# Gate and up products of a feed-forward layer: nine of eleven steps by seven block products in place of eight

## The reference, cut to what matters

```python
D_FF = 2816
h2 = rms_norm_2(x, g_ffn[layer])                              # 512 x 1024
x = x + (jax.nn.silu(h2 @ w_ffn_gate[layer])                  # 1024 x 2816
         * (h2 @ w_ffn_up[layer])) @ w_ffn_down[layer]
return rms_norm_2(x, g_final)
```

## Time and profile before

| | |
|---|---|
| median of 3 runs | 1060.87 us (1060.67 to 1061.41) |
| the profiled execution | 1061.1 us |
| its span, from first to last instruction | 1059.3 us |
| PE busy in the span | 1049.7 us |
| DVE, ACT, POOL busy | 509.0, 448.8, 400.2 us |
| mean granted TensorE clock | 0.999 of full speed |

### The profile page before, as it was taken

The page is one execution under the profiler, slowest core; times in us unless marked ns, Lnnn a source line. Parts: engine busy times, 40 slices in busy tenths (PEclk is TensorE's granted clock), DMA queues, the critical chain, the costliest instruction groups (busy, mean ns, idle before and its releaser), DMA issues.

```text
span 1059.3 us, 14455 instructions
## 1 busy us (share of the span) xinstructions
PE 1049.7 (99%) x5545; PEld 844.1 (80%) x5545; DVE 509.0 (48%) x1061; ACT 448.8 (42%) x788; POOL 400.2 (38%) x300
## 2 busy tenths in 40 slices
PE   9999999999999999999999999999999999999997
PEld 8877897767678876888777888888888888888886
DVE  6766788875752316998587344230000000032444
ACT  6444457676653425233465414342221221233533
POOL 3455520001025333446000255434435354465772
PEclk9999999999999999999999999999999999999999
DMA  9541141201032331332221232223232323323221
GB/s 298 184 120 51 34 119 41 75 17 44 28 120 80 72 117 43 101 99 80 80 80 41 80 104 95 91 77 110 80 118 79 114 84 104 114 80 100 82 97 80
DMA packets 84724, 95.72 MB, mean 90 GB/s; under 512 B 8121, under 2 KB 70930, under 8 KB 84666
## 3 DMA queue, kind: packets, MB, share of 16 engines
q1 hardware_dynamic: 83706, 92.46, 28.0%
q0 software_dynamic: 560, 2.12, 0.6%
q10 hardware_dynamic: 400, 0.35, 0.1%
HBM read 92.80 MB, written 2.12 MB: 90 GB/s over the span
## 4 chain that ended last, share of the span: by engine, by line
PE 94%; DVE 4%; ACT 1%; issue 1%; POOL 0%; DVEq 0%; ACTq 0%; POOLq 0%
PE bank L1882 56%; PE bank L2194 23%; PE bank L1940 4%; PE bank L1971 3%; PE bank L2012 3%; PE bank L1988 1%; DVE L L1478 1%; PE bank L2169 1%; PE bank L1833 1%; PE bank L2098 1%; PE bank L2045 1%; DVE L L1524 1%; DVE pool L1483 0%; PE bank L2001 0%; PE bank L1964 0%
## 5 line engine op out<-in xcount | busy, mean ns | idle before, releaser
L1042 POOL TENSOR_TENSOR w_lo<-raw,w_hi 128x512 fp32r<-128x512 f32 (+1 forms) x190 | 267.2, 1436 | 415.7 <-ACT w_hi L1104 403.0
L1882 PE MATMUL bank<-h_hi,w_hi 128*128 128x512 f32 (+1 forms) x560 | 224.0, 400 | 0.3 <-ACT h_hi L1315 0.2
L1882 PE MATMUL bank<-h_hi,w_lo 128*128 128x512 f32 (+1 forms) x560 | 218.6, 390 | 0.0
L1882 PE MATMUL bank<-h_lo,w_hi 128*128 128x512 f32 (+1 forms) x560 | 217.8, 390 | 0.0
L1082 POOL TENSOR_TENSOR w_lo<-raw,w_hi 128x512 fp32r<-128x512 f32 x88 | 110.7, 1290 | 133.5 <-ACT w_hi L1353 67.1
L1104 ACT ACTIVATE w_hi<-raw 128x512 fp32r<-128x512 f32 (+3 forms) x94 | 111.2, 1213 | 116.1 <-PE bank L1882 113.8
L1882 PE MATMUL bank<-w_hi,h_hi 128*128 128x512 f32 (+2 forms) x397 | 145.3, 366 | 0.0
L1882 PE MATMUL bank<-w_lo,h_hi 128*128 128x512 f32 (+2 forms) x397 | 144.5, 364 | 0.0
L1882 PE MATMUL bank<-w_hi,h_lo 128*128 128x512 f32 (+2 forms) x397 | 144.5, 364 | 0.0
L2194 PE MATMUL bank<-h_hi,w_hi 128*128 128x512 f32 x352 | 137.1, 389 | 0.0
L2194 PE MATMUL bank<-h_hi,w_lo 128*128 128x512 f32 x352 | 137.0, 389 | 0.0
(11 more groups left out here) (213 smaller groups left out, 1260.3 us busy)
## 6 DMA issues: line engine op xcount, KB each, us to landing
raw<-in_w_in SPq DMA_DIRECT2D x29, 1024.0 KB, 5.3
raw<-in_w_ffn_gate SPq DMA_DIRECT2D x11, 1024.0 KB, 5.4
raw<-in_w_ffn_up SPq DMA_DIRECT2D x11, 1024.0 KB, 5.4
raw<-in_w_out SPq DMA_DIRECT2D x8, 1024.0 KB, 5.0
raw<-in_w_ffn_down SPq DMA_DIRECT2D x8, 1024.0 KB, 5.1
raw<-in_w_in SPq DMA_DIRECT2D x8, 512.0 KB, 4.6
pool<-in_cmp_w SPq DMA_DIRECT2D x4, 1024.0 KB, 9.1
raw<-in_w_ffn_down SPq DMA_DIRECT2D x4, 768.0 KB, 4.3
```

The costliest lines, as they stand in the source:

```text
L1042: nc.gpsimd.tensor_tensor(w_lo[:, u.n % 2, cols], raw[:, u.n % 2, cols], w_hi[:, u.n % 2, cols].bitcast(F32), ALU.subtract).then_inc(lo_do ...
L1882: ins = mm(bank[t.bank][0:t.m, 0:u.width if u.token else T], stationary, moving, start=first and n == 0, stop=last and n == len(products) ...
```

## The change

Two of the eleven steps stay as they are ("plain", the first and the last). The nine between are made by Strassen's scheme in Winograd's form, seven block products in place of eight. For one step and one of the two matrices, the 1024 features are cut in halves, the 256 columns in two blocks of 128 and the 512 tokens in two halves of 256: a 2 x 2 product of blocks, eight products of (512 features x 128 columns) by (512 features x 256 tokens). The scheme forms four sums of weight blocks and four sums of token blocks, makes seven products and adds these up differently. Gate and up give 14 products a step, each 4 blocks of features x 3 = 12 matmuls with 256 moving columns. In detail:
- **Token sums**, once: DVE adds `h_hi` and `h_lo` to one array, forms four sums of blocks, ACT makes their high parts and DVE their low parts (`token_sums_of_h`, `token_low`).
- **Weight sums**, in each fast step: POOL makes eight sums of 512 columns (`weight_sums`), six of them in place in `raw`, two into `PT`.
- **High and low parts**: ACT makes 14 high parts of 512 columns a step (`high`), DVE all 14 low parts (`split_fast`); both go into rings of seven pieces in `w_hi` and `w_lo`, so they run up to seven products ahead of PE. POOL makes low parts in the plain steps only.
- **Loads**: weights lie in memory in blocks as the stage needs them (the host array is reordered); SP loads eight blocks of 256 KB a fast step, each as soon as the low part that was the last to read its place in `raw` is done.
- **Merging**: the products go to banks 0 to 7; ACT moves four of them to SBUF, DVE makes eight sums and three multiplications a step (`merge`), ACT three SiLUs.

The diff, cut to its core. The steps and the table of a fast step's products (matrix, weight block or `None` for the sum in `PT`, number of the product), and how many weight sums each needs:

```diff
+    PLAIN_STEPS = 2
+    FAST_STEPS = FFN_STEPS - PLAIN_STEPS
...
+        A11, A12, A21, A22 = range(4)
+        GATE, UP = range(2)
+        fast = [(GATE, A12, 2), (UP, A12, 2), (GATE, A11, 1), (UP, A11, 1), (GATE, A21, 5), (UP, A21, 5), (GATE, A11, 6), (UP, A11, 6),
+                (GATE, A12, 3), (GATE, None, 7), (UP, None, 7), (UP, A12, 3), (GATE, A22, 4), (UP, A22, 4)]
+        FAST, RING, MERGES, WEIGHT_SUMS = len(fast), 7, 11, 8
+        def sums_before(i):
+            return {4: 2, 5: 4, 6: 5, 7: 6, 8: 7, 9: 1, 10: 3, 11: 8}.get(i, 0)
```

SP's loads:

```diff
+            plain_load(0, 0)
+            for j in range(2):
+                sp.wait_ge(lo_done, order[n0 + j].lo_end)
+                for b in (A12, A11, A21, A22):
+                    load_block(0, j, b)
+            with sp.Fori(0, FAST_STEPS - 1) as f:
+                for i in (6, 7, 8, 11, 12, 13):
+                    j = fast[i][0]
+                    sp.wait_ge(*lo_at(f, i))
+                    for b in {6: (A21,), 7: (A21,), 8: (A12, A11), 11: (A12, A11), 12: (A22,), 13: (A22,)}[i]:
+                        load_block(f + 1, j, b)
```

POOL's sums:

```diff
+                        if i in (4, 5):
+                            for b in (A11, A21, A22):
+                                pool_e.wait_ge(block_in[j][b], f * 16 + 16)
...
+                            nc.gpsimd.tensor_tensor(PT[:, j, :], w11, w21, ALU.subtract).then_inc(weight_sum, 1)
+                            pool_e.wait_ge(weight_sum, n + (2 * j + 1))
+                            nc.gpsimd.tensor_tensor(w21, w21, w22, ALU.add).then_inc(weight_sum, 1)
+                        if i in (6, 7):
+                            pool_e.wait_ge(weight_sum, n + (2 * j + 2))
+                            pool_e.wait_ge(*lo_at(f, 2 + j))
+                            nc.gpsimd.tensor_tensor(w11, w21, w11, ALU.subtract).then_inc(weight_sum, 1)
+                        if i in (8, 11):
+                            pool_e.wait_ge(weight_sum, n + (5 + j))
+                            pool_e.wait_ge(*lo_at(f, j))
+                            nc.gpsimd.tensor_tensor(w12, w12, w11, ALU.subtract).then_inc(weight_sum, 1)
```

ACT's order in a fast step:

```diff
+                    def fast_step(f, last=False):
+                        for p in range(FAST):
+                            if p in (0, 1, 4, 5):
+                                sc.wait_ge(product_done, f * FAST + (p + 1))
...
+                            if p == 13:
+                                sc.wait_ge(product_done, f * FAST + 13)
+                                act_fn(L[:, 4, 0:256], bank[4][:, 0:256], ACT.Silu).then_inc(fast_silu, 1)
+                            if p + RING < FAST:
+                                high(f, p + RING)
+                            elif not last:
+                                high(f + 1, p + RING - FAST)
```

DVE's low parts, and their order among the merges:

```diff
+                    def split_fast(f, i):
+                        j, b, _ = fast[i]
+                        ve.wait_ge(fast_hi, f * FAST + (i + 1))
+                        v.tensor_tensor(ring(w_lo, i), weight_block(j, b), ring(w_hi, i).bitcast(F32), ALU.subtract)\
+                            .then_inc(fast_lo, 1)
...
+                        for p in range(FAST):
+                            merge(f, p)
+                            if p + RING < FAST:
+                                split_fast(f, p + RING)
+                            elif not last:
+                                split_fast(f + 1, p + RING - FAST)
```

PE's products:

```diff
+                    def fast_step(f):
+                        for i, (j, _, m) in enumerate(fast):
+                            pe.wait_ge(*lo_at(f, i))
+                            if i == 2:
+                                pe.wait_ge(fast_silu, f * 3 + 1)
+                            if i == 3:
+                                pe.wait_ge(merged_done, f * MERGES + 1)
...
+                            for k in range(4):
+                                for w, x in ((w_hi, x_hi), (w_hi, x_lo), (w_lo, x_hi)):
+                                    ins = mm(dst[:, 0:256], ring(w, i)[:, P * k:P * k + P], x[:, k, :],
+                                             start=n == 0 and m in (1, 2, 3, 5), stop=n == 11, skip_group_check=True)
```

More of the change, by code:

```diff
@@ new lines, in _ @@
+                    up_hi(0)
+                    gates(0)
+                    act_fn(st[:, ST_RS + NT:ST_RS + NT + 1], eps, ACT.Copy).then_inc(fast_silu, 1)
+                    for t in (3, 1, 2, 4):
+                        sc.wait_ge(t_sum, {3: 1, 1: 2, 2: 3, 4: 4}[t])
+                        sc.wait_ge(tile_done, ffn_last.done)
+                        act_fn(token_sum(t, 0), t_f32[t], ACT.Copy).then_inc(t_hi, 1)
+                    for i in range(RING):
+                        high(0, i, first=True)
@@ new lines, in _ @@
+                    with sc.Fori(0, FAST_STEPS - 1) as f:
+                        fast_step(f)
+                    fast_step(FAST_STEPS - 1, last=True)
+                    sc.wait_ge(raw_in[n0 % 2], ffn_u[2].arrived)
+                    sc.wait_ge(product_done, FAST * (FAST_STEPS - 1) + 11)
+                    act_fn(w_hi[:, n0 % 2, :], raw[:, n0 % 2, :], ACT.Copy).then_inc(hi_done, 1)
+                    up_hi(1)
+                    gates(1)
+                    sc.wait_ge(raw_in[n0 % 2], ffn_u[2].arrived + 16)
@@ L1367, in _ @@
+                    sc.wait_ge(tile_done, t0 + 6)
+                    act_fn(w_hi[:, n0 % 2, :], raw[:, n0 % 2, :], ACT.Copy).then_inc(hi_done, 1)
                     split_act_hi(down_u[0])
@@ new lines, in fast_step @@
+                    def fast_step(f, last=False):
+                        for p in range(FAST):
[4 more added lines that the diff above has]
+                                split_fast(f + 1, p + RING - FAST)
+                    token_sums_of_h()
+                    for j in range(2):
+                        gated(0, j, act[:, j, :])
+                    v.memset(st[:, ST_LAM:ST_LAM + 1], 0.0).then_inc(merged_done, 1)
@@ L1824, in _ @@
+                    token_low()
+                    for i in range(RING):
+                        split_fast(0, i)
+                    with ve.Fori(0, FAST_STEPS - 1) as f:
+                        fast_step(f)
+                    fast_step(FAST_STEPS - 1, last=True)
+                    gated(PLAIN_STEPS - 1, 0, act[:, NFF - 2, :])
                     split_act_lo(down_u[0])
-                    gated(FFN_STEPS - 1, 1, act[:, NFF - 1, :])
+                    gated(PLAIN_STEPS - 1, 1, act[:, NFF - 1, :])
```

208 lines of the change are left out of this document (170 added, 38 removed).

## The result

The changed kernel takes 1069.07 us (median of 4 runs, 1068.79 to 1070.53) against 1060.8 of before beside it: 1.008 times as long, 95% interval 1.0062 to 1.0097, 8.3 us slower. The forecast was 1066.1, in the range 1056.5 to 1076, slower with 0.63.

A forecast was written before the change was run, and what follows sets the result against it. The prediction took TensorE's matmuls to bound the stage. Nine fast steps -5.9, start +7.3, clock +1.3 and end +2.5 made +5.2 us on 1060.9, so 1066.1 us, range 1056.5 to 1076.

The forecast's parts named there:

- TensorE's floor: Fast step's 168 matmuls at 119.6 ns take 20.09 us against 21.76, at most 15.0 us gained in nine steps.
- The circle: Fast step's loop of load, POOL's sums and DVE's rest: 21.1 us, so nine steps gain 5.9 us; chance 0.70.
- the load with its queue: From low part 12 freeing a 256 KB block to its reload landing: 3.8 us, bounds 2.7 and 4.9.
- the eight sums: POOL's eight weight sums in a fast step, 1.60 to 1.65 us each beside DVE's low parts: 13.0 us.
- DVE behind them: After the eighth sum, DVE's rest of low part 7, low parts 8 to 12 and two merges: 4.3 us.
- Where TensorE waits: In a fast step, about 1 us of waits at products 2 and 3, for multiplications on DVE.
- the rival that hides the circle: Sums and low parts miss each other, circle under 20.1 us, nine steps gain 15.0, total 1057.0 us; chance 0.20.
- The start: Ahead of the first fast product, TensorE waits for DVE's token sums and low parts: 7.3 us late (6.2 to 8.5).
- The clock: Behind the start gap the granted clock falls; the way back costs 1.3 us, at most 1.9.
- The end: Ahead of the last plain step, last SiLU, ACT's high copy and POOL's first low part cost TensorE 2.5 us.
- Fetch: Rival: the longer fast loop is fetched anew at eight returns, 3.9 us each, 31 us, total 1097; chance 0.05.
- whole-instruction turns: Rival: sum and low part exclude each other fully, 1.98 us a pair, circle 23.9 us, total 1091; chance 0.05.

The follow-up runs named there:

- e7_short_lows: Changed kernel with DVE's low parts of products 4 to 8 and 11 made for only 32 of 512 columns; 1061.79 us (one run).
- e12_early_a11: e8_three_orders with POOL making both sums that don't read A22 first, and block A11 loaded once the last sum has read it; 1062.74 us.
- e6_first_sum_twice: Changed kernel with POOL making the first gate sum of every fast step twice; 1079.49 us (one run).
- e1_first_sum: Changed kernel with POOL's first sum of a matrix no longer waiting for block A22, which it doesn't read; 1066.54 us.
- e11_best: e12_early_a11 with e4_copy_early, an earlier wait for the last plain step, a reordered start with first up blocks loaded singly, and earlier first-step merges; 1056.04 us.
- e8_three_orders: Changed kernel with the edits of e1_first_sum and e2_silu_early, plus DVE's multiplication of product 13 ahead of low part 5; 1066.63 us.
- e3_start_order: Changed kernel with DVE's first weight low parts ahead of or between the token lows, and TensorE waiting for each token low singly; 1069.22 us.
- e4_copy_early: Changed kernel with ACT copying the last plain step's gate weights' high part ahead of the last SiLU; 1066.10 us.
- e2_silu_early: Changed kernel with ACT's SiLU of product 12 one place earlier, ahead of the high part of product 5; 1069.26 us.

## Why the prediction was right, step by step

- **TensorE's floor.** 119.6 ns a matmul and 20.09 us a step: after, the matmuls of a product start 0.12 us apart, with the others out of the way a step was 20.28 (e7_short_lows), and steps without any wait take 20.16 (five in a row in e12_early_a11). Right.
- **The circle.** 21.1 forecast, 21.36 measured, and on the circle that was named (e6_first_sum_twice, e1_first_sum). Its three terms: the load with its queue 3.8 forecast, and 741.19 - 736.22 = 5.0 measured, just over the upper bound of 4.9 (the load itself 4.06, where I took 3.3 between rows of 2.7 and 3.9); the eight sums 13.0, and 741.17 to 754.63, 13.5; DVE behind them 4.3, and 754.63 to 757.66, 3.0. Low part 8, not 7, was all but done when the eighth sum was. The first term and the last were mis-sized in opposite directions, by 1.2 and 1.3. The path was right; that its sum came within 0.3 us is luck.

The last sums and DVE's low parts after, the timeline that answers to the earlier trace rows:

```profile
748.06 3.17 POOL L1161 TENSOR_TENSOR raw<-raw 128x512 f32<-128x512 f32 x2
751.18 3.45 POOL L1165 TENSOR_TENSOR raw<-raw 128x512 f32<-128x512 f32 x2
...
753.63 1.55 DVE L1981 TENSOR_TENSOR w_lo<-raw,w_hi 128x512 fp32r<-128x512 f32 x1 [0.15 <-ACT w_hi L1462]
755.10 0.41 DVE L1991 TENSOR_TENSOR L<-bank,L 128x256 f32<-128x256 f32 x1
```

- **Where TensorE waits.** Only half right: product 2 for ACT's SiLU, which stands behind the high part that needs the fourth sum, and product 6 for the first merge, not products 2 and 3 for multiplications. Those come next (e1_first_sum).
- **A bound that was left out.** The price of taking turns was charged to POOL's sums alone. DVE pays it too: 16 instructions with both inputs in SBUF at 0.61 and nine of 256 columns at 0.34 (start to start) are 12.8 us; if eight of them meet a sum and last 1.70, 8 x 1.09 = 8.7 more, 21.5 us, over TensorE's 20.09 by itself. That is an estimate for the worst case; 19.3 of 21.44 was measured in the changed kernel (749.09 to 770.53) and 19.9 of 20.97 in e11_best. So the rival that hides the circle, at 1057.0, needs more than a shorter circle: of the 1.27 us a step over the floor, the edits to loads, sums and orders brought back 0.3 to 0.6 in the steps with waits. Steps of 20.16 occur between them (e8_three_orders, e12_early_a11, e11_best), so the floor can be reached; what decides is open.
- **The start.** 7.3 us forecast, 8.07 measured, on another path. DVE's eight token sums were not slowed (0.61 apart); POOL was. The 1024-column sums took 2.2 us each, not 1.45. They and the first gated product were over at 713.1, and DVE then stood idle for 3.04 us, until the plain step's end let the second gated product go: the case that the prediction priced at 6.2. The other 1.8 us are the token lows, 1.75 each on the mean (two of 1.22, two of 2.29 beside POOL's sums), not 1.22: the price of turns, once more. The timeline that answers to the earlier trace rows:

```profile
699.54 11.85 POOL L1143 TENSOR_TENSOR w_lo<-raw,w_hi 128x512 fp32r<-128x512 f32 x4 [13.46 <-ACT w_hi L1443]
...
698.62 4.90 DVE L1962 TENSOR_TENSOR pool<-h_hi,h_lo 128x512 f32<-128x512 f32 x8
703.56 2.19 DVE L1965 TENSOR_TENSOR pool<-pool 128x1024 f32<-128x1024 f32 x1
...
716.12 0.69 DVE L1957 TENSOR_TENSOR pool<-bank,L 128x512 f32<-128x512 f32 x1 [3.04 <-PE bank L2415]
...
717.87 5.62 DVE L1976 TENSOR_TENSOR token_sums<-pool,token_sums 128x1024 fp32r<-128x1024 f32 x3
...
724.15 0.58 PE L2446 MATMUL bank<-h_hi,w_hi 128*128 128x256 f32 x1 [8.07 <-DVE w_lo L1981]
```

  As a cost by itself the gap was wrong, though the sum came out: e3_start_order took it away and kept the time.
- **The clock.** 1.3 forecast. From 724.53 to 727.09 twelve steps from start to start take 0.213 us each in place of 0.12, 1.1 us, and the first start is late by 0.26: 1.4. That this is so near is luck. The 20 small matmuls that were to bound it run at a granted clock of 1.00 (before, 1 to 6 us), so their 0.23 us has another reason; and in e4_copy_early, whose start is the same, product 2 comes 0.8 us later behind the first start, so the cost is not the same in every execution.
- **The end.** 2.5 forecast, 2.27 measured. That the stall can also lower the clock, 1.5 us where it does, was not in it.
- **Fetch and whole-instruction turns.** No gap at the loop's returns. A pair took 1.71 (751.92 to 753.63 between two low parts), as the earlier trace rows had it, so the step did not go to 23.9; but the 32-column low part that lasts as long as a sum shows that DVE can wait for a whole instruction of POOL's. The Trainium skill, page "SBUF — State Buffer", section "Who interferes with whom", has this lock; the traces agree in that wait (1.28 us in place of 0.19), not in a pair that costs the sum of both (1.71, not 1.29 + 0.69).
- **The sum.** From the traces: nine steps and the clock -3.3 (192.57 from the first product to the end of the last, for 195.84), the start +8.2, the end +2.4, the last plain step +0.1: +7.5, against +5.2. Of the 2.3 us, 1.3 are steps longer than 21.1 and the first fast step, 0.9 the start.

## What to carry over

Where two engines take turns at the same memory, add the price of the turns to the busy time of both over a whole period, before looking for the circle: the change had room on each engine alone and little on the two together. When one limit is cut, price the next before promising the difference; here it lay 0.6 us a step below. A gap at the head of a stage is worth only what the engines behind it can deliver sooner: price their work up to the first product that needs all of it, not the gap.

## What was not expected of the hardware

- **POOL held off for eight instructions.** The four low parts that took POOL 5.02 us before took 11.85 after. The first of them started at 699.54 and the second at 704.62, while DVE ran eight two-input instructions 0.61 us apart until 703.5; in the fast steps, where each of DVE's low parts first waits for its high part, the two alternate. That the waits between are what lets POOL in was not tested.
- **On DVE the price is by instruction more than by size.** 32 columns beside a sum last 1.28 us, 512 columns 1.55 to 1.78. POOL's sum does gain by the shorter company: 1.3 us in place of 1.6.
- **A stall of 2.27 us** was followed by a granted clock of about half, the lower level, in four traces of nine (0.54 in e2_silu_early, 0.50 in e6_first_sum_twice, 0.53 in e12_early_a11, and e7_short_lows) and not in the others (1.00 after), with nearly the same work ahead of it.
- **One loop, two paces.** 21.0 us a step, and later steps without a wait, in one execution of e11_best; in e12_early_a11 it is the other way round, five steps without a wait and then three of 21.0. The instructions are the same, and which of DVE's meet which sums differs; what tips a step from one pace to the other was not tested.
